# A new order of the head groups within a lane, in a fused one-core hybrid attention block

## What is computed

```python
o_a = _rmsnorm(_diff_attention(qa, ka, va, rel_bias, lam)) * (1.0 - lam_init)   # 4 heads x two softmaxes, T5 bias
o_b = _stick_breaking(sb_q, sb_k, sb_v)                                        # 8 heads
o_c = _forgetting_attention(f_q, f_k, f_v, log_f)                              # 8 heads
o_m = _memory_attention(m_q, km, vm)                                           # 4 heads over 256 memory rows
y = concat(o_a, o_b, o_c, o_m) * silu(gate)
x = x + _rmsnorm(y @ w_out, post_norm)
```

## Time and profile before

| what | value |
|---|---|
| median of 3 runs | 2693.18 us (2689.74 to 2699.65) |
| profiled execution, from first to last instruction | 2698.7 us |
| PE busy over that span | 2434.9 us, 90% |
| DVE, ACT, POOL busy | 1794.7, 1618.4, 1344.0 us |
| mean granted clock of TensorE | 0.976 |
| DMA queue 1 (SP's), share of 16 engines | 62.7% |

### The profile page before, as it was taken

How to read it: one execution, slowest core, us unless ns; L and a number is a source line. 1 busy time by engine, 2 the same in 40 slices (tenths; PEclk the granted TensorE clock), 3 DMA queues, 4 the chain that set the end, 5 groups by cost and what they waited for, 6 DMA issues and landing times. The chain is left out here.

```text
span 2698.7 us, 73492 instructions
## 1 busy us (share of the span) xinstructions
PE 2434.9 (90%) x27422; PEld 1663.8 (62%) x27422; DVE 1794.7 (67%) x4993; ACT 1618.4 (60%) x4437; POOL 1344.0 (50%) x2128
## 2 busy tenths in 40 slices
PE   5699999997899999998999999989999998599998
PEld 4576666665676676666666666667666666344443
DVE  7657989755489897755798887647998865211111
ACT  5456865566678765676677656776776567411121
POOL 6423457676435576774245766752557667400000
PEclk9799999999999999999999999999999999799999
DMA  6346875388759753888598546994885469963331
GB/s 199 98 100 126 140 141 110 72 171 155 146 116 161 144 108 85 165 155 158 107 163 141 108 100 145 164 169 105 157 147 109 98 123 164 203 192 101 94 110 47
DMA packets 942750, 357.38 MB, mean 132 GB/s; under 512 B 768292, under 2 KB 927148, under 8 KB 942380
## 3 DMA queue, kind: packets, MB, share of 16 engines
q1 hardware_dynamic: 935800, 334.83, 62.7%
q0 software_dynamic: 6592, 17.83, 2.5%
HBM read 89.22 MB, written 35.23 MB: 46 GB/s over the span
## 5 line engine op out<-in xcount | busy, mean ns | idle before, releaser
L1507 POOL TENSOR_TENSOR rows<-rows 128x512 f16<-128x512 f32 (+3 forms) x864 | 868.9, 1019 | 786.5 <-ACT rows L1442 782.9
L1271 PE MATMUL job<-wt,big 128*128 128x128 f16 x10752 | 672.8, 221 | 17.8 <-DVE gate_s L1597 13.6
L1271 PE MATMUL job<-big,wt 128*128 128x512 f16 x2688 | 665.3, 381 | 15.2 <-DVE planes L1518 6.1
L1271 PEld LDWEIGHTS job<-wt,big 128*128 128x128 f16 x10752 | 631.1, 99 | 66.5 <-DVE gate_s L1597 19.3
L1442 ACT CAST rows<-rows 128x512 f16<-128x512 f32 (+3 forms) x864 | 464.0, 547 | 230.5 <-DMA rows<-rows 138.6
L1332 PE MATMUL mixed<-values,rows 128*128 128x64 f16 (+1 forms) x8544 | 439.5, 202 | 108.2 <-DMA rows<-rows 83.5
L1332 PEld LDWEIGHTS mixed<-values,rows 128*128 128x128 f16 x8544 | 381.8, 100 | 240.2 <-DMA rows<-rows 121.6
L1454 ACT ACTIVATE rows<-rows,neg_max 128x512 f32<-128x512 f32 (+3 forms) x704 | 447.1, 637 | 88.4 <-DVE neg_max L1564 84.4
L1556 DVE TENSOR_SCALAR_CACHE_REDUCE rows<-scores 128x512 f32<-128x512 f32 (+3 forms) x704 | 399.9, 588 | 129.3 <-POOL rows L1507 99.6
L1317 PE MATMUL scores<-stack 128*128 128x512 f16 (+3 forms) x1600 | 439.0, 350 | 50.1 <-DVE rows L1556 43.0
L1271 PEld LDWEIGHTS job<-big,wt 128*128 128x128 f16 x2688 | 246.3, 98 | 254.3 <-issue 14.0
(11 more groups left out here) (160 smaller groups left out, 2986.2 us busy)
## 6 DMA issues: line engine op xcount, KB each, us to landing
stack<-planes SPq DMA_DIRECT2D x160, 192.0 KB
ws<-w_in SPq DMA_DIRECT2D x56, 512.0 KB, 4.7
y_halves<-y_out_halves SPq DMA_DIRECT2D x64, 256.0 KB, 2.8
rows<-rows SPq DMA_TRANSPOSE x864, 3.3
rows<-x SPq DMA_DIRECT2D x16, 512.0 KB, 5.8
temps<-w_out POOLq DMA_DIRECT2D x64, 128.0 KB, 3.2
out_weight_halves<-temps POOLq DMA_DIRECT2D x64, 128.0 KB, 3.6
planes<-y_halves SPq DMA_DIRECT2D x8, 1024.0 KB, 8.5
```

The costliest lines, as they stand in the source:

```text
L1271: last = nc.tensor.matmul(dst, lhs, rhs, start=(k0 == 0 and q == 0), stop=(k1 == KT and q == len(pairs) - 1))
L1507: nc.gpsimd.tensor_tensor(halves_of(tau, 1, w), scored(plan.chunk_at(g, m, k0), 0, w), halves_of(tau, 0, w), ALU.subtract).then_inc(low_po ...
```

## The change

The units of a lane run as memory, forgetting, stick-breaking, differential, and the value slots follow suit. All 64 pieces of the output weight are put into the first three differential units (21, 21 and 22), so the last one has none. The planner gets new ranks and `AHEAD` by kind, and it models how long the DMA engines themselves are taken (`DMA_TIME`, `DMA_LAG`): each DMA occupies one shared resource in turn, and lands after that. The `sums` DMA now waits for the stick-breaking unit of the lane before, three units earlier, and for nothing in the first lane. `known`, `missing` and `taken` only make the planner faster. No instruction's work is changed.

```diff
+DMA_TIME = {"turn": 0.39, "strip": 2.1, "store": 1.05, "stacks": 0.7, "sums": 0.3, "pairs": 1.0, "near_in": 0.5}
+DMA_LAG = {"turn": 0.75, "strip": 1.7, "store": 1.0, "stacks": 1.5, "sums": 1.5, "pairs": 1.0, "near_in": 1.5}
-KIND_ORDER = ("mem", "stick", "diff", "forget")
+KIND_ORDER = ("mem", "forget", "stick", "diff")
 RANK = {   # all numbers new; of those in the text:
-    "pe": {"gate": -0.69350, "mix": 0.82372, "score": 2.95609, "y": 4.31887, "project": 6.43835},
+    "pe": {"gate": -0.31704, "mix": 0.09117, "score": 1.70262, "y": 3.53853, "project": 4.61336},
...
-AHEAD = {0: 0.74778, 1: 0.51500, 2: 0.48997, 3: 0.66327}
-SLACK, LATE = 3.79816, 7.63635
+AHEAD = {"mem": 0.95294, "stick": 0.51500, "diff": 0.10702, "forget": 0.55547}
+SLACK, LATE = 3.17600, 8.22475
...
     Unit(lane, "mem", 3, 1, float(PAIR_W) ** -0.5),
-    Unit(lane, "stick", 1, 0, HEAD_DIM ** -0.5),
-    Unit(lane, "diff", 0, 1, HEAD_DIM ** -0.5),
     Unit(lane, "forget", 2, 0, HEAD_DIM ** -0.5),
+    Unit(lane, "stick", 1, 1, HEAD_DIM ** -0.5),
+    Unit(lane, "diff", 0, 0, HEAD_DIM ** -0.5),
...
-        each = self.wo_tiles * self.wo_cuts // len(diffs)
-        for at, t in enumerate(diffs):
-            self.pieces[t] = list(range(at * each, (at + 1) * each))
+        turns, total = len(diffs) - 1, self.wo_tiles * self.wo_cuts
+        for at, t in enumerate(diffs[:turns]):
+            self.pieces[t] = list(range(at * total // turns, (at + 1) * total // turns))
...
                     if n == self.first_chunk[t]:
                         need.append(("exp", n - 1))
-                        if t > len(KIND_ORDER):
-                            need.append(("score", self.first_chunk[t - 1] - 1))
...
-                need = [("weigh", self.last_chunk[t - 2] - 1)]
+                need = [("score", self.last_chunk[t - 2] - 1)] if t >= len(KIND_ORDER) else []
                 q["sums"].append((("sums", t), ("sums", t), need, 0.55, 2.5))
...
             free[e] = at + length
             end[key], on[key] = at + length + lag, e
+            if name in DMA_TIME:
+                engines = max(engines, at + 0.9) + DMA_TIME[name] * (op[2][3] if name == "turn" else 1)
+                end[key] = engines + DMA_LAG[name]
...
-                        sp.wait_ge(weighed, plan.stick_at[plan.last_chunk[t - 2] - 1] + 1)
+                        if t >= len(KIND_ORDER):
+                            sp.wait_ge(weighed, plan.stick_at[plan.last_chunk[t - 3] - 1] + 1)
                         sp.dma_start(hk_c[64:67], c_dram[:, 2 * lane:2 * lane + 2, :]).then_inc(c_landed, 16)
```

More of the change, by code:

```diff
@@ L51 @@
 EASY = 2.0
+DMA_TIME = {"turn": 0.39, "strip": 2.1, "store": 1.05, "stacks": 0.7, "sums": 0.3, "pairs": 1.0, "near_in": 0.5}
+DMA_LAG = {"turn": 0.75, "strip": 1.7, "store": 1.0, "stacks": 1.5, "sums": 1.5, "pairs": 1.0, "near_in": 1.5}
 ENGINES = ("pe", "act", "dve", "pool", "sp")
-KIND_ORDER = ("mem", "stick", "diff", "forget")
+KIND_ORDER = ("mem", "forget", "stick", "diff")
 RANK = {
-    "pe": {"gate": -0.69350, "mix": 0.82372, "score": 2.95609, "y": 4.31887, "project": 6.43835},
[L56 to L62, removed]
-}
-AHEAD = {0: 0.74778, 1: 0.51500, 2: 0.48997, 3: 0.66327}
-SLACK, LATE = 3.79816, 7.63635
+    "pe": {"gate": -0.31704, "mix": 0.09117, "score": 1.70262, "y": 3.53853, "project": 4.61336},
+    "act": {"take": -2.38532, "beta": 4.38613, "job": 5.70697, "hi": 6.03616, "convert": 6.69913,
+            "stick": 7.44656, "exp": 8.19356},
+    "dve": {"weigh": -0.89989, "lo_dve": 0.28667, "low": 4.94274, "combine": 5.13788, "post": 5.65863,
+            "scan": 5.96151, "copy": 6.71535, "widen": 6.82195, "near": 7.31231},
+    "pool": {"lo": 1.70131, "wo": 2.00000, "root": 3.13577},
+    "sp": {"sums": 3.76762, "turn": 4.13062, "stacks": 4.59029, "near_in": 5.94116, "store": 6.71303,
+            "strip": 7.71714, "pairs": 8.67044},
+}
+AHEAD = {"mem": 0.95294, "stick": 0.51500, "diff": 0.10702, "forget": 0.55547}
+SLACK, LATE = 3.17600, 8.22475
 DVE_LOW = {"mem": 0, "stick": 0, "diff": 0, "forget": 0}
@@ L184, in __init__ @@
             first = next(n for n in self.stick_n if n >= self.first_chunk[t - 1] and self.slots[n][0] + 1 == SLOTS)
-            self.slot_turn[first] = (at + 1) * each
+            self.slot_turn[first] = (at + 1) * total // turns
         self.converts = [(0, G)]
@@ L367, in queues @@
             if unit.kind == "diff":
-                for p in self.pieces[t]:
+                for p in self.pieces.get(t, []):
                     need = [("wo_lo", p - 1)] if p else []
@@ L395, in run @@
         free["sp"] = 0.6
+        engines = 0.0
         opened, done, jobs, part = None, 0.0, 0, 0
@@ L401, in run, with ready @@
                 "g": self.k_tiles // 2 * 3 * P * PE_ROW}
-        def ready(e, task):
+        known, missing = {}, {}
+        def ready(e, name, task):
+            if name in known:
+                return known[name]
+            if missing.get(name) is not None and missing[name] not in end:
+                return None
             at = 0.0
@@ L406, in ready, with taken @@
                 if key not in end:
+                    missing[name] = key
                     return None
                 at = max(at, end[key] + (HOP if on.get(key) != e else SAME))
+            known[name] = at
             return at
+        def taken(name):
+            known.pop(name, None)
+            missing.pop(name, None)
+            return q[name].popleft()
         while any(q.values()) or opened:
@@ L420, in run @@
                     task = q[name][0]
-                    at = ready(e, task)
+                    at = ready(e, name, task)
                     if at is None:
@@ L447, in run @@
             if name in ("gate", "project"):
-                what, t, kind, index = q[name].popleft()[1]
+                what, t, kind, index = taken(name)[1]
                 opened, part = (jobs, "g" if what == "gate" else what, t, kind, index), 0
@@ L526, in marks @@
             x += sum(each[g] for g in range(t * nt, t * nt + nt))
-            ahead = AHEAD[(t + 1) % len(KIND_ORDER)] * work[t + 1] if t + 1 < len(UNIT) else 0.0
+            ahead = AHEAD[UNIT[t + 1].kind] * work[t + 1] if t + 1 < len(UNIT) else 0.0
             marks.append((x, sum(work[:t + 1]) + ahead))
```

2 lines of the change are left out of this document (1 added, 1 removed).

## The result

The change made the kernel slower. Its median is 2734.23 us (four runs, 2729.8 to 2739.32) against 2692.22 us (four runs, 2689.74 to 2699.65) on the same chip: a ratio of 1.0144, 95% interval 1.0124 to 1.0164, so +1.4% or 42 us where 36 us less was forecast. It is outside the forecast range. The profiled execution spans 2727.9 us against 2698.7. The one after is the fastest of its four, and the span before is longer than the times of three of the four, so the two traces hold 29 us of the 42.

A forecast was written before the change was run, and what follows sets the result against it. PE, busy 2434.9 of 2698.7 us, was taken as the bound, with DMA pacing forgetting units. Idle-time terms -34 + 12 - 15 - 3 + 4 = -36 us gave a median of 2657, range 2615 to 2705.

The forecast's parts named there:

- Where PE idles, and that stick-breaking behind would fill it: Forgetting units of lanes one to three: stick-breaking projection behind them cuts PE idle from 26.5, 20.9, 16.0 to 9.7, 9.8, 9.4 us.
- forgetting units of lanes one to three: PE idles 34 us less there, with 74 us of projection behind in place of 24.5; bounds nothing and 63.
- differential units of lanes one to three: With only memory's projection behind, their ends run dry at times: 4 us more PE idle a lane, 12 in all.
- last lane: Ending in differential, not forgetting: 505 us against 533.8, 29 less, or nothing less; the middle, 15 us less, taken.
- The forgetting unit that moved forward takes its 150: Last lane: the forgetting unit, now second, is taken at 150 us within the lane's 505.
- The unit shrinks by what moved out until DVE stops it: Differential units of lanes one to three: could run in 152 us at 93% DVE share, 20 less than now.
- Clock: Forgetting units: filled gaps win back part of PE's time at 1.2 GHz, 3 us; bounds 0 and 21.
- Pieces, table loads: Output weight pieces in the first three differential units cost nothing; table loads stay at 4 and 4.
- The seam to stick-breaking: Forgetting to stick-breaking: first sigmoid waits for a longer last exp; 1 us a lane taken, 4 in all.
- Slower: Rival, chance 0.15: late row ring lengthens stick-breaking units, 4 x 19.8 = 79 us less the 36, about 2736.
- Nothing to measure: Rival, chance 0.17: DMA paces the forgetting unit, filler is missing at differential ends; within 13.5 us, about 2686.
- The two signs that the prediction itself gave for being wrong: Differential units' last steps show PE idle at 1.2 GHz; the last take-out comes no earlier than 2344.

## Why the prediction was wrong, step by step

- **Where PE idles, and that stick-breaking behind would fill it: right.** 9.7, 9.8 and 9.4 us of idle time were forecast for the three forgetting units, 10.3, 9.0 and 9.7 came; TensorE's clock stayed at 2.4 GHz in all of them.

The prediction counts in PE's idle time, and so its sum can be set against the traces, cut by the same take-outs:

| term, change of PE's idle time in us | forecast | measured |
|---|---|---|
| forgetting units of lanes one to three | -34 | -34.5 |
| differential units of lanes one to three | +12 | +38.0 |
| last lane | -15 | +16.8 |
| stick-breaking units of lanes one to three | +4 | +4.7 |

With -1.0 in the other memory units and the start, +0.2 in the last stage and 4.8 us more of busy PE that makes the 29 us between the spans. The clock, forecast at -3 in the sum, has no row: it would show in PE's busy time. The second and the third term failed; the first came, but not the length that the text tied to it.

- **"The forgetting unit that moved forward takes its 150": the first step that failed.** The idle time went, but in a longer unit. The text took the unit as 150 us of DMA with PE work to be slipped in for nothing, though 132 us of PE work and 26 more are 158 already. It took 186, 167, 166 and 170. What the runs show in its place: 26 us more PE work bring PE to 95% there, and PE and DMA then pace it together (of 18 us of longer front end 6 go when PE is unloaded, 4.5 when DMA is, 13 with both, an estimated 10 of them owed to the change). Some 3 to 5 go with the restacks, which also moved into it; the runs don't say whether these lie within DMA's part or beside it. What the rest is, 3 to 8 us, was not shown.

- **"The unit shrinks by what moved out until DVE stops it": the step that decided.** It put the differential unit at 152 us or more by DVE's busy share and the last one at 133. It stayed at 171.8, and the last one at 162.4. The failing term is "4 us a lane, 12 in all", which came to 38. Neither PE nor a busy share sets the unit's length: it is 172 us with PE at 115 or at 162 us. Of what was tried with the lists unchanged, only less work in the inverse root made it shorter, by 10 us in two lanes, and 1.4 and 3.6 in the first and last. The rest of its length, copy to exp to combine to the next copy, is read from the timeline. The 11 us a lane that were to come out here are missing in full, and so is the last lane's gain: it took 552.6 us (2372.5 - 1819.9) where 505 was forecast, 29 of the 48 too much in its differential unit and 20 in its forgetting one.

- **Clock: wrong in sign, and of no weight.** 80.0 us at 1.2 GHz in these two kinds of unit became 103.2, all in differential ones. The Trainium skill (TensorE: Matmul & The Clock Gate, Terms) would charge the time at the lower level times the share lost, by which an estimate gives 12 us more for the change. The differential unit measures 172 us at a granted clock of 1.00, 0.95 and 0.83, so here it charges nothing: PE isn't what is waited for.

- **Pieces, table loads: right.** Pieces 0.1%; the exp and the sigmoid line load their tables 4 and 4 times, as before.

- **The seam to stick-breaking, 4 us: the size came, the cause was not looked for.** Stick-breaking units of lanes two to four took 162 to 164 us in place of 166 to 168, since they too hold less PE work, but PE idles 3 to 6 us more in each. No run shows whether that is the seam.

- **The rivals.** "Slower" had the right sign and 2736 us, close to the 2734 measured, by the wrong mechanism: it named stick-breaking units 20 us longer, and they got shorter. "Nothing to measure" named half the truth, that DMA holds the forgetting unit and that the filler is missing at the differential ends; it took the differential unit to have room. The two signs that the prediction itself gave for being wrong, differential ends idle at 1.2 GHz and a last take-out no earlier than 2344, both came.

Open: how much the order costs by itself. Its effect is +3.0% with one set of planner numbers and -0.3% with the other, and no experiment could hold the lists fixed, since the lists are made from the order. Lists better suited to the new order stay a rival for a part of the loss.

## What to carry to other kernels

A busy share below 90% is not room. Before work is moved out of a stage to shorten it, follow one period of that stage from a step's last instruction to the next step's; where one link follows the other, moving other work away may give nothing while the stage that receives it grows. Cutting the moved kind of work out of both kernels tells this in one run each: here the differential unit stayed at 172 us in both. And an idle time that is filled is a gain only if the stage's length is set elsewhere than by what the filler loads.

## What the runs showed of the hardware

POOL's small operations on 128x1 are not of one price. In a differential step of the kernel after they take 0.19 us alone, and the same ones 0.58 or 0.59 while DVE runs its combine (POOL's timeline; the combine starts at 1247.54):

```profile
1247.48 0.19 POOL L1488 TENSOR_TENSOR root<-root,sc 128x1 f32<-128x1 f32 x1
1247.76 0.59 POOL L1490 TENSOR_SCALAR root<-root 128x1 f32<-128x1 f32 x1
1248.43 0.58 POOL L1492 TENSOR_TENSOR root<-root 128x1 f32<-128x1 f32 x1
1249.09 0.58 POOL L1486 TENSOR_TENSOR root<-root 128x1 f32<-128x1 f32 x1
1249.75 0.58 POOL L1488 TENSOR_TENSOR root<-root,sc 128x1 f32<-128x1 f32 x1
1250.42 0.19 POOL L1490 TENSOR_SCALAR root<-root 128x1 f32<-128x1 f32 x1
```

The 13 operations take 5.0 us there, from 1246.12 to 1251.1, and DVE, beside whose combine they are slow, then waits for them. It isn't DVE being busy as such. Over the whole trace of the kernel after, the root's operations that ran wholly beside a copy of scores, which reads PSUM, took 0.19 to 0.20 us, all 292 of them, as much as the 128 beside no DVE work. Of the 85 wholly beside a 512-wide combine, both of whose inputs are rows in SBUF, 69 took over 0.3 us, with a median of 0.58 over all 85. The Trainium skill (GPSIMD Engine Reference, Architecture) says that GpSimd's read and write ports are shared with DVE; the rows agree, though no run here separated the port from another cause. That the third Newton step runs beside the combine may be why leaving out one of three gains nearly as much as leaving out all; this is argued, not shown.

Halving the bytes of the transposes lowered the DMA share of a unit from 0.91 to 0.56 and its length by 3% (153.1 to 148.0 us): a DMA share of 91% was no proof that DMA alone set the pace.
